# The output projection's third token tile: the next-to-last weight unit's products moved ahead of the last unit's, and an expert load moved up with its release

## The reference, cut to what matters

```
z = rms_norm(x, g1) @ w_in               # then convolution, RG-LRU, spatial gating
merged = sigmoid(gate_a) * ya + sigmoid(gate_b) * yb
x = x + merged @ w_out                   # the product that the change reorders
logits = rms_norm(x, g2) @ w_router + b_router
top 4 of 32 experts per token, softmax of the 4 logits
x = x + sum over the 4 of gate * (swiglu(h @ w_gate_up[e] + b) @ w_down[e] + b)
y = rms_norm(x, g_final)
```

## Time and profile before

| what | value |
|---|---|
| time, median of 3 runs | 1228.41 us (1227.81 to 1228.77) |
| time of the profiled execution | 1227.76 us |
| its span, first to last instruction | 1226.2 us |
| outside the span | 1.56 us |
| mean granted TensorE clock | 0.989 of full |
| bytes moved | 443.70 MB |
| busy: PE / DVE / ACT / POOL | 96% / 32% / 18% / 7% of the span |

### The profile page before, as it was taken

How to read it: one execution, slowest core, us unless ns; L and a number is a source line. 1 busy time by engine, 2 the same in 40 slices (tenths; PEclk the granted TensorE clock), 3 DMA queues, 4 the chain that set the end, 5 groups by cost and what they waited for, 6 DMA issues and landing times.

```text
span 1226.2 us, 16203 instructions
## 1 busy us (share of the span) xinstructions
PE 1183.0 (96%) x6491; PEld 672.0 (55%) x6491; DVE 394.2 (32%) x648; ACT 224.7 (18%) x386; POOL 81.6 (7%) x243
## 2 busy tenths in 40 slices
PE   9999999999999999799999989999999998999996
PEld 8999999985435354243434343535435343543532
DVE  4648586756243413021211111221212121221222
ACT  5533772233101010000101010101101010110111
POOL 4100000010201001101100010101001010110000
PEclk9999999999999999899999999999999999999999
DMA  7543226598999999999999999999999999999994
GB/s 230 170 157 113 93 104 253 188 341 343 410 427 426 428 426 425 410 428 426 424 429 426 426 425 421 421 425 426 427 426 427 426 427 428 427 423 428 427 421 168
DMA packets 54591, 443.70 MB, mean 362 GB/s; under 512 B 5324, under 2 KB 5420, under 8 KB 23536
## 3 DMA queue, kind: packets, MB, share of 16 engines
q1 hardware_dynamic: 53152, 439.91, 87.0%
q0 software_dynamic: 1216, 2.68, 1.0%
q10 hardware_dynamic: 144, 0.04, 0.0%
HBM read 440.63 MB, written 1.98 MB: 361 GB/s over the span
## 4 chain that ended last, share of the span: by engine, by line
PE 84%; DMA 13%; issue 2%; DVE 1%; POOLq 0%; ACT 0%; POOL 0%; DVEq 0%; SPq 0%; ACTq 0%
PE ps L1663 29%; PE ps L1725 18%; DMA wexp<-in_w_gate_up_dram 10%; PE ps L1561 8%; PE ps L1300 7%; PE ps L1301 7%; PE ps L1302 7%; DMA wexp_low<-in_w_down_dram 2%; PE ps L1577 2%; PE ps L1578 1%; PE ps L1611 1%; PE ps L1406 1%; PE ps L1569 1%; PE ps L1675 1%; PE ps L1523 0%
## 5 line engine op out<-in xcount | busy, mean ns | idle before, releaser
L1663 PE MATMUL ps<-wexp,xt 128*64 128x512 f32 (+1 forms) x2048 | 464.0, 604 | 19.0 <-DMA wexp<-in_w_gate_up_dram 12.6
L1663 PEld LDWEIGHTS ps<-wexp,xt 128*64 128x64 f32 (+1 forms) x2048 | 145.4, 133 | 265.2 <-issue 264.5
L1725 PE MATMUL ps<-wexp,act_t 128*64 128x512 f32 (+1 forms) x1104 | 227.2, 593 | 5.6 <-issue 4.2
L1725 PEld LDWEIGHTS ps<-wexp,act_t 128*64 128x64 f32 (+1 forms) x1104 | 81.5, 131 | 136.5 <-issue 136.4
L1215 DVE TENSOR_TENSOR y<-y,ps 128x1024 f32<-128x1024 f32 x51 | 60.7, 1218 | 210.6 <-PE ps L1578 208.6
L794 ACT ACTIVATE g<-g 128x512 f32<-128x512 f32 x33 | 20.8, 630 | 547.9 <-DVE g L1229 547.9
L1300 PE MATMUL ps<-act_h,split 128*128 128x384 f32 x352 | 117.9, 335 | 0.0
L1302 PE MATMUL ps<-act_h,split 128*128 128x384 f32 x352 | 117.6, 334 | 0.0
L1301 PE MATMUL ps<-act_l,split 128*128 128x384 f32 x352 | 117.6, 334 | 0.0
L1561 PEld LDWEIGHTS ps<-pick,xn 128*128 128x128 f32 x768 | 91.1, 196 | 14.8 <-issue 14.8
L1561 PE MATMUL ps<-pick,xn 128*128 128x128 f32 x768 | 94.1, 283 | 1.7 <-POOL pick L561 1.7
(11 more groups left out here) (315 smaller groups left out, 972.5 us busy)
## 6 DMA issues: line engine op xcount, KB each, us to landing
wexp<-in_w_gate_up_dram SPq DMA_DIRECT2D x92, 2048.0 KB, 24.6
wexp<-in_w_down_dram SPq DMA_DIRECT2D x48, 2048.0 KB, 27.0
wexp<-in_w_gate_up_dram SPq DMA_DIRECT2D x38, 1024.0 KB, 24.5
wexp<-in_w_down_dram SPq DMA_DIRECT2D x20, 1024.0 KB, 12.0
raw<-in_w_in_dram SPq DMA_DIRECT2D x19, 1024.0 KB, 5.1
wexp_low<-in_w_gate_up_dram SPq DMA_DIRECT2D x17, 1024.0 KB, 24.4
wexp_high<-in_w_gate_up_dram SPq DMA_DIRECT2D x16, 1024.0 KB, 23.0
wexp_low<-in_w_down_dram SPq DMA_DIRECT2D x5, 1024.0 KB, 23.1
```

What stands on the lines that cost most here:

```text
L1663: i_ = pe.matmul(ps[s0:s0 + w, b, :], xt[:, k, s0:s0 + w], weights(k, x)[:, at_:at_ + UC], start=k == 0, stop=k == CB - 1)
L1725: i_ = pe.matmul(ps[s0:s0 + w, 6 + c, :], act_, weights(CB + m, x)[:, D * kk + UC * c:D * kk + UC * c + UC], start=k == 0, stop=k == CB - 1)
```

## The change

PE: the four groups of `mix_tokens(1, 0, 2)` (unit 28, tile 2) stood in two pairs behind `turn_tokens(1, 0)` and `turn_tokens(1, 1)`. Now they stand together ahead of `mix_tokens(1, 1, 0)`. The four groups of `mix_tokens(1, 1, 2)` (unit 29, tile 2) each move up: one behind `turn_tokens(1, 0)`, one behind `turn_tokens(1, 1)`, one behind `router_strips(1, 2)`, and one behind the logits. None is left between `count_before(0)` and `count_before(1)`. SP: the wait for `MIX_U - 1` and load 11 move ahead of the wait for the stores and the load of `beside`. Load 13 stays behind `beside`; it no longer has a wait of its own. No instruction is added or removed.

```diff
+            sp.wait_ge(unit_used, MIX_U - 1)
+            load_expert(11)
             sp.wait_ge(stored, 5 * 16)
             sp.dma_start(beside[:], exp_one(BESIDE % 2, BESIDE // 2)).then_inc(beside_landed, 16)
-            sp.wait_ge(unit_used, MIX_U - 1)
-            load_expert(11)
             load_expert(13)
             sp.wait_ge(unit_used, MIX_U)
...
             for t in range(TT):
                 turn_tokens(0, t)
+            mix_tokens(1, 0, 2)
             mix_tokens(1, 1, 0)
...
             router_strips(0, TT)
             mix_tokens(1, 1, 1)
             turn_tokens(1, 0)
-            mix_tokens(1, 0, 2, range(0, 2))
+            mix_tokens(1, 1, 2, range(0, 1))
             turn_tokens(1, 1)
-            mix_tokens(1, 0, 2, range(2, 4))
+            mix_tokens(1, 1, 2, range(1, 2))
             pe.wait_ge(yt_ready, TT + 2)
             router_strips(1, 2).then_inc(quarters_mm, 1)
-            mix_tokens(1, 1, 2, range(0, 1))
+            mix_tokens(1, 1, 2, range(2, 3))
             pe.wait_ge(quarters_ready, 1)
...
-            mix_tokens(1, 1, 2, range(1, 2))
-            mix_tokens(1, 1, 2, range(2, 3))
+            mix_tokens(1, 1, 2, range(3, 4))
...
             count_before(0)
-            mix_tokens(1, 1, 2, range(3, 4))
             count_before(1)
```

## The result

The changed kernel takes 1229.76 us (median of 20 runs, 1228.96 to 1233.11), the kernel before 1228.16 (20 runs, 1226.35 to 1229.83). The ratio is 1.0015, 95% interval 1.0009 to 1.0021: slower by 1.8 us (1.1 to 2.6). The forecast was 1230.7 us, 2.3 slower, in a range of 1228.3 to 1232.6. The change costs time, by less than the 0.2% that was taken as the bound of "the same". The profiled execution took 1229.02 us, its span is 1227.5.

What follows compares the result with a forecast made beforehand. The weight stream, started by PE's first pass, was taken to bound the kernel. SP part 0, work ahead +1.4, stall +0.85, idle pieces 0 gave +2.25, rounded to 2.3: 1228.41 + 2.3 = 1230.7 us, range 1228.3 to 1232.6.

Steps and rivals of the forecast that it cites:

- The SP part is worth 0: Loads 11 and 13 go out about 7 us earlier, but PE's use of ring slots limits later loads: 0 us.
- Two groups more ahead of the strips, 1.4 us: Between the twelve transposes and router_strips(1, 2) PE has 14 groups instead of 12, at 0.69 us each: +1.4 us.
- The stall of 0.85 us at the strips for `evacuate_turned(1, 1)`: With thinner filling, PE waits before router_strips(1, 2) for ACT's copy: +0.85 us.
- The later idle pieces cost nothing: Between logits and `pick` of tile 0, PE idles about 1.3 us in pieces while DVE sets the pace: 0 us.
- rival 3: New PE waits drop the clock to 1.2 GHz for about 3.4 us, losing 1.7 us: 1232.4 us or more; chance 0.09.
- One to one to the end: Each microsecond by which PE's first pass starts later, from 290.96 us, is one at the end: 2.25 us here.
- the stream's start at 311 us sets the end: DMA engines are full from 311 to 1200 us at 425 GB/s, so the weight stream's start, bytes and rate fix the end.
- waiting 30 us for a weight load at 622.8 us: The prediction's reading of the chain: PE, having used the ring's stock, waits for loads from about 620 us on.

Runs made afterwards that it cites:

- e2_sp_only: The kernel before with only SP's new order, PE's order unchanged; `beside` goes out some 7 us later: 1227.93 us, ratio 0.9996 (0.9987 to 1.0005).
- g2_root_filled: The changed kernel with ACT's square root moved behind evacuate_turned(1, 1) and 5 unused products between count_before(0) and count_before(1): 1228.57 us, ratio 1.0005.
- e1_pe_only: The kernel before with only the PE reordering, SP's order as before: 1230.59 us, ratio 1.0021 (1.0012 to 1.003).
- e6_spin_second: The kernel before with 28 unused 128x128 products on PE ahead of the second pass: 1232.92 us, ratio 1.0043 (1.003 to 1.0057).
- f4_spin_sixth: The kernel before with 28 unused 128x128 products on PE ahead of the sixth pass: 1228.36 us, ratio 1.0 (0.9991 to 1.0009).
- e4_ids_first: The kernel before with SP's reading of the second pass's expert numbers moved ahead of load 18: 1228.52 us, ratio 1.0001 (0.9991 to 1.001).

## Why the prediction was right

Point by point, by its own steps:

- **The SP part is worth 0.** Borne out: in the changed kernel the two loads leave a hole at 295 us, and the bytes moved 190 us behind the start of the first pass differ by 0.07 MB. `e2_sp_only`, where no load is earlier, adds that SP's order alone makes no difference. "DMA: Bandwidth & Descriptors" of the Trainium skill, section "Rules for kernel authors", says to issue a DMA early; here that gave nothing, as the number of slots was the limit.
- **Two groups more ahead of the strips, 1.4 us.** 1.39 in `g2_root_filled`, where nothing else is left, as a distance; its time, +0.6 us (-0.5 to +1.7), doesn't show it by itself.
- **The stall of 0.85 us at the strips for `evacuate_turned(1, 1)`.** 0.79 us in the changed profile, 0.80 when it was taken away.
- **The later idle pieces cost nothing.** True for the path as such. But they are what rival 3 needed: in two of four profiles the clock fell behind them, at 1.6 us each time. "TensorE: Matmul & The Clock Gate" in the Trainium skill, section "Why this matters for your kernels", warns of idle gaps; the profile of `e1_pe_only` agrees in that its clock fell behind such gaps, none of which reached 0.9 us, while the changed kernel's own profile, with the same gaps, kept its clock.
- **One to one to the end.** Right in effect: 2.18 us at the first pass, 1.8 (1.1 to 2.6) at the end, and 6.25 for 5.5 (3.9 to 7.2). The reason that I gave was not. I wrote that the stream's start at 311 us sets the end and that nothing behind it hangs on PE. In fact PE sets the pace from the transposes to 483 us, and in the last 192 us of that it waits for no load; only the stream behind the second gate runs by itself. `e6_spin_second` and `f4_spin_sixth` show this, and the bytes of `e4_ids_first` agree. The prediction also has PE "waiting 30 us for a weight load at 622.8 us"; that is the load's way from issue to landing, and the longest wait of PE for a load before 660 us is 2.70. The mistake was to read a window of 889 us whose average of 425 GB/s covers a dip of 6 us, and not to ask in each pass what SP's next load waits for. The forecast survived it since both gates move with PE.

The measured loss is 0.5 us under the forecast in the ratio. The distances allow 2.18 where the clock holds and 3.8 where it falls, so the middle of the measurement is rather low for them; its interval holds 2.18, and which part of the executions meets the low clock stays open.

## What to carry to other kernels

When work is moved between the steps of a chain over several engines, count two things for each step: the work now ahead of it, and whether the filling behind the step before still covers the other engines' time. Filling that is moved forward can be paid twice: here two groups cost 1.4 us as work ahead and the gap that they left 0.8 as a stall, while two more that were missing further on lengthened nothing. A transfer that goes out earlier gains only if the next one may follow; with a ring, look for what the first load beyond the ring waits for. Before calling a stretch bound by the stream, look at it in windows of a few microseconds, and at every gate of the issuing queue: an average over the whole stretch hides the place where the stock runs out. And compare kernels by the bytes moved at a fixed distance from the same event: one profile each tells 0.6 us here, where the times of 11 executions leave 1.1 open.

## What was unexpected of the hardware

The clock fell to 1.2 GHz behind waits none of which reached 0.9 us, in two of four profiles with such waits open, though a single wait of 1.47 us elsewhere left it alone. A 128x128 product of float32 costs 0.22 us in a row (6.25 / 28), a transpose of the same size 0.11 (1.31 / 12). The stream repeats well, 393.90 to 394.16 MB moved 800 us behind the first pass's start in eleven profiles with the ring of before (all but `e6_spin_second`). Yet the landing of the last load that PE waits for scatters from 713.1 to 715.7 us behind the fifth pass's first load over all twelve, more than the effect that was to be measured, while PE's stretch repeats to some hundredths.
